# Hybrid DeltaNet, pooling and expert block on one core: input transposed raw as it lands, output products grouped by shape

## The chip, the core and the metric

The kernel runs on one core of a Trainium2 chip. The number that counts is the device time of one execution in microseconds, as the median of several runs. The profile of one execution gives what each engine did: TensorE (PE, with its weight loads as PEld), VectorE (DVE), ScalarE (ACT), GpSimd (POOL), and SyncE (SP), which only issues transfers here.

## What is computed

`x` is 512 tokens by 1024 values, float32. The parts of the reference that the change touches are the first norm and projection, and the output of the scan:

```python
h = _rmsnorm(x, attn_norm_w[l])        # x * rsqrt(mean(x*x) + eps) * w
proj = h @ w_in[l]                     # 1024 -> 2568: q, k, v, z, two gates, pool input
...
def step(state, inp):                  # 8 chunks of 64 tokens, 4 heads of 128
    qd, kd, u_c, w_c, qk_c, gt = inp
    v_new = u_c - jnp.einsum('bhid,bhde->bhie', w_c, state)
    o = jnp.einsum('bhid,bhde->bhie', qd, state) + jnp.einsum('bhij,bhje->bhie', qk_c, v_new)
    state = state * gt[..., None, None] + jnp.einsum('bhid,bhie->bhde', kd, v_new)
    return state, o
```

Before the scan, q, k and v go through a causal convolution of 4 taps, silu and norms, and a unit lower triangular 64x64 matrix per head and chunk is inverted (the "transposed inverse" below is kept as tiles TR and TM and built in 5 levels). Behind the scan come an output norm and gate, the output projection `w_out`, a second norm, a router that picks 4 of 32 experts for each token, the experts (1024 -> 2048 -> 1024 with a clamped SwiGLU), the weighted sum and a last norm.

## The kernel before

Everything is float32 apart from the gather matrices of the experts. Each engine has its own hand-written program; the order of the calls in the code is the order on the engine, and semaphores tie the engines together. SP's queue carries all loads.

**Start.** SP issues the four loads of `x` (128 tokens each, into `xs`), then seven small loads of parameters into the 61 rows of `prow` (norm weight, four rows of convolution taps, two more), and then the weights of the input projection in pieces of 1 MB. ACT sums the squares of each block of tokens (L566) and takes one root for all four (L568). DVE first builds masks for the inverse (L786 to L803: six of them, `lvl`, and `icnt`), copies the transposed parameters out of PSUM (`pcol`, L806), inverts the roots (L808), and scales the four blocks of x into `xn` (L810). PE transposes the parameters (L1235) and then, once all four blocks are scaled, `xn` in 32 tiles of 128x128 (L1240), eight PSUM banks of 512 tokens. ACT (L572) and DVE (L813) share the eight copies out of PSUM and multiply by the norm weight of each row: that is `hT`, the transposed normed input.

**Projections and inverse.** `project(m)` (L1256) multiplies 8 weight tiles of 128x128 with the 8 rows of `hT` into bank 0 or 1, m = 0 to 19. Ahead of `project(0)` stands `four_chunks` (L1285), the two gates of each head, whose sums by chunk follow at L1453. ACT copies a projection out with the first tap (L576, `tap`), DVE adds three taps (L831, `conv`), ACT applies silu (L581). The gates go through a chain of small operations on DVE (L852 to L870) with exponentials and a logarithm on ACT (L645 to L651). The products and the levels of the inverse stand between the projections on PE, written out by hand.

**Scan.** For chunks n = 1 to 7 PE runs `state_values(n)` (L1376), `outputs(n - 1)` and `state_change(n)` (L1390) with quarters of projections between them. DVE subtracts (`values`, L970), updates the state (`state`, L983 and L985) and adds the decayed part to the output (`output`, L996); ACT copies the other part of the output (`keep_intra`, L632). `outputs(n)` makes for each of four heads two products: the queries with the state (L1405: 128 rows of contraction, 64 columns of weights) and the chunk's own scores with the new values (L1406: 64 rows, 64 columns). They alternate head by head. Each float32 product is two instructions in the trace.

**Tail.** Output projection (L1276), second norm, router, then the loop over blocks of 32 tokens of one expert: gather (L1603), gate and up (L1641), down (L1662), with 1 MB units of weights in a ring of 20 slots that SP refills as PE frees them. One unit of the ring is filled early wherever the scan has given its place back.

Of the kernel before, what the change touches and what calls it, by code (L numbers as in the profile page):

```python
# [18 lines left out]
P = 128  # L19
D = 1024  # L20
T = 512
TB = T // P
KD = D // P
H = 4
CONV = 4
# [26 lines left out]
def moe_block(nc, x, attn_norm_w, w_in, conv_w, a_log, dt_bias, dn_norm_w, pool_w, pool_scale, w_out,  # L52
# [3 lines left out]
    with ctx:  # L56
# [66 lines left out]
        catT = cat[:, :].rearrange("p (k t) -> p k t", k=KD)  # L123
        xn = cat[:, :].rearrange("p (b d) -> p b d", b=TB)
        DX = cat[:, 0:1024].rearrange("p (c f) -> p c f", c=NC)
# [92 lines left out]
        def bc(v, n, at):  # L218
# [11 lines left out]
            "iota_ok", "const_ok", "lvl_ok", "pool_step", "pool_mix", "bias_ok")]  # L230
        std_ok, xn_ok, pcol_ps, pcol_ok, xt_ps, ht_even, ht_odd = [sem(n) for n in (
            "std_ok", "xn_ok", "pcol_ps", "pcol_ok", "xt_ps", "ht_even", "ht_odd")]
        proj_ps, tap_ok, conv_ok, silu_ok, ba_ps, dve_step = [sem(n) for n in (
# [83 lines left out]
        def _(sp):  # L317
            def param(row, n, src):
                sp.dma_start(prow[row:row + n, :], src).then_inc(par_in, 16)
# [3 lines left out]
            param(NANW, KD, attn_norm_w.rearrange("l (k p) -> (l k) p", p=P))  # L323
            for j in range(CONV):
                param(NCV + NQKV * j, NQKV, conv_w[0, j:j + 1, :].rearrange("l (k p) -> (l k) p", p=P))
            param(NDN, 1, dn_norm_w)
            param(NPS, 4, pool_scale.rearrange("l (k p) -> (l k) p", p=P))

            w_in_v = w_in[0].rearrange("(k p) c -> p k c", p=P)
# [227 lines left out]
        def _(act):  # L557
# [3 lines left out]
            def row(v):  # L561
                return v.rearrange("p a t -> p (a t)")

            for b in range(TB):
# [209 lines left out]
        def _(dve):  # L774
# [3 lines left out]
            def step(ins, s, count):  # L778
# [17 lines left out]
                                        op0=ALU.mult, op1=ALU.subtract))  # L796
            for s in range(1, LEVELS + 1):
# [4 lines left out]
            link(V.tensor_scalar(icnt[:, :], iotaf[:, 0:PAD], 1.0, None, ALU.add))  # L802
            step(V.reciprocal(icnt[:, :], icnt[:, :]), lvl_ok, 1)  # L803

            dve.wait_ge(pcol_ps, 1)
            step(V.tensor_copy(pcol[:, :], ps[:, 7, 0:61]), pcol_ok, 1)  # L806
            dve.wait_ge(std_ok, 1)
            link(V.reciprocal(sm[:, 8:12], sm[:, 4:8]))  # L808
            for b in range(TB):
                V.tensor_scalar(xn[:, b, :], xs[:, b, :], sm[:, 8 + b:9 + b], None, ALU.mult).then_inc(xn_ok, 1)  # L810
            for k in range(1, KD, 2):
                dve.wait_ge(xt_ps, k + 1)
                V.tensor_scalar(hT[:, k, :], bank(k), pcol[:, NANW + k:NANW + k + 1], None, ALU.mult).then_inc(ht_odd, 1)  # L813

# [24 lines left out]
            for hh in range(2):  # L839
                r = slice(CH * hh, CH * (hh + 1))  # L840
                link(V.tensor_copy(bch[r], bcr[r, 0:2 * H].rearrange("p (k a b) -> p k a b", k=2, a=2)[:, :, :, hh]))
            dve.wait_ge(part_ps, 1)
            V.tensor_copy(ba_part, bank(6)).then_inc(part_ok, 1)
            conv(0)

            dve.wait_ge(ba_ps, 1)
# [384 lines left out]
        def _(pe):  # L1231
            mm, tr = nc.tensor.matmul, nc.tensor.transpose
            pe.wait_ge(const_ok, 6)
            pe.wait_ge(par_in, 16 * (3 + CONV))
            tr(ps[:, 7, 0:61], prow[:, :], ident[0:61, 0:61]).then_inc(pcol_ps, 1)  # L1235
            pe.wait_ge(pcol_ok, 1)
            pe.wait_ge(xn_ok, TB)
            for k in range(KD):
                for b in range(TB):
                    last = tr(bank(k)[:, b * P:(b + 1) * P], xn[:, b, k * P:(k + 1) * P], ident)  # L1240
                last.then_inc(xt_ps, 1)
            pe.wait_ge(ht_even, KD // 2)
            pe.wait_ge(ht_odd, KD // 2)

            def project(m, lo=0, hi=KD):

                piece = m // 2
                if lo == 0:
                    if m % 2 == 0:
                        pe.wait_ge(win_in[piece % 3], (piece // 3 + 1) * 16)  # L1250
                    if 2 <= m < NQKV + 2:
                        pe.wait_ge(conv_ok, m - 1)
                    elif m >= NQKV + 2:
                        pe.wait_ge(silu_ok, m - 1)
                for k in range(lo, hi):
                    last = mm(bank(m % 2), win[:, piece % 3, k, m % 2 * P:(m % 2 + 1) * P], hT[:, k, :], start=k == 0,  # L1256
                              stop=k == KD - 1)
                if hi == KD:
                    last.then_inc(proj_ps, 1)
# [133 lines left out]
            def outputs(n):  # L1393

                if n == 0:
                    pe.wait_ge(u_ok, 4)
                    pe.wait_ge(qkt_ok, 2)
                else:
                    pe.wait_ge(vn_ok, n)
                    pe.wait_ge(o_ok, n)  # L1400
                for hp in range(2):
                    for hh in range(2):
                        c, h = 2 * n + hp, 2 * hp + hh
# [30 lines left out]
            def h2_transposed(b):  # L1434
# [3 lines left out]
                for half in range(2):  # L1438
# [5 lines left out]
                    last.then_inc(h2t_ps, 1)  # L1444

            pe.wait_ge(wba_in, 16)
            four_chunks(bank(6), wba, hT, part_ps)
            project(0)
            pe.wait_ge(const_ok, 7)
# [5 lines left out]
            last.then_inc(ba_ps, 1)  # L1455
            project(1)
            project(2)
# [240 lines left out]
```

## Time and profile before

| | us |
|---|---|
| median of 3 runs | 1402.07 (1401.7 to 1402.2) |
| profiled execution, its own time | 1397.82 |
| its span in the trace | 1396.0 |
| mean granted clock of TensorE | 0.965 of full |
| PE busy | 1272.8 (91%) |
| DVE busy | 504.8 (36%) |
| ACT busy | 289.1 (21%) |
| POOL busy | 159.5 (11%) |

The profiled execution has 1.82 us around its span, and lies 4.25 us under the median of the timed runs. Times in the trace count from the start of the span. The stages: x and norm to 21 us, projections and inverse to 190 us, scan to 254 us, output projection and second norm to 313 us, router to 353 us, experts to about 1350 us, sum and last norm to the end. A busy share says little for such a kernel, since each stage has another limit; what counts is which wait or engine ends last in the stage.

### The profile page before, as it was taken

The numbers are of one execution on the slowest core, as the hardware profiler recorded it, in microseconds if no ns is written. First come the engines' busy times: TensorE is split into PE (matmuls) and PEld (weight loads), VectorE is DVE, ScalarE is ACT, GpSimd is POOL, SyncE is SP. The second block draws the span as 40 slices with busy tenths as digits, with TensorE's granted clock in tenths as the row PEclk, the third lists the DMA queues.
The fourth block names the chain that finished last, engine by engine and source line by source line (L and its number), as shares of the span: only waits on it lengthen the run. The fifth ranks groups of instructions, "written<-read, shape, count | busy, mean of one in ns | idle before, by whom it ended". The sixth has DMA issues, their size and how long they took to land.

```text
span 1396.0 us, 52461 instructions
## 1 busy us (share of the span) xinstructions
PE 1272.8 (91%) x21747; PEld 750.5 (54%) x21747; DVE 504.8 (36%) x1624; ACT 289.1 (21%) x494; POOL 159.5 (11%) x256
## 2 busy tenths in 40 slices
PE   5999999983998999999999999999999999988860
PEld 3446654441555665566565556556566656554440
DVE  5454223226333333333333333333333333332227
ACT  3431123123111111211121112121121112111102
POOL 3100420006000001100010101010010001100000
PEclk9999999995999999999999999999999999999985
DMA  6212140418199999999999999999999999999956
GB/s 209 78 61 62 31 165 32 151 37 352 60 410 416 406 417 407 417 405 418 398 403 417 401 417 407 417 406 417 405 401 417 394 418 404 417 419 417 416 199 293
DMA packets 94579, 447.27 MB, mean 320 GB/s; under 512 B 10973, under 2 KB 22706, under 8 KB 61194
## 3 DMA queue, kind: packets, MB, share of 16 engines
q1 hardware_dynamic: 90778, 437.34, 77.8%
q0 software_dynamic: 3696, 8.40, 1.6%
q8 instruction: 82, 1.34, 0.4%
q14 instruction: 23, 0.19, 0.0%
HBM read 432.52 MB, written 14.88 MB: 320 GB/s over the span
## 4 chain that ended last, share of the span: by engine, by line
PE 69%; DMA 25%; DVE 4%; issue 1%; ACT 0%; SPq 0%; DVEq 0%; POOLq 0%; ACTq 0%
PE ps L1641 27%; DMA ring<-in_w_gate_up_dram 16%; PE ps L1662 13%; PE ps L1256 10%; DMA ring<-in_w_down_dram 8%; PE ps L1603 5%; PE ps L1276 4%; PE ps L1323 1%; DVE ring L1217 1%; PE ps L1634 1%; PE ps L1653 1%; PE ps L1406 1%; PE ps L1612 1%; PE ps L1405 1%; DMA ring<-pair_rows_dram 1%
## 5 line engine op out<-in xcount | busy, mean ns | idle before, releaser
L1641 PE MATMUL ps<-ring,cat 128*32 128x256 f32 x9856 | 555.1, 383 | 15.9 <-DMA ring<-in_w_gate_up_dram 15.9
L1641 PEld LDWEIGHTS ps<-ring,cat 128*32 128x32 f32 x9856 | 311.1, 111 | 231.2 <-DMA ring<-in_w_gate_up_dram 20.7
L1662 PE MATMUL ps<-ring,cat 128*32 128x256 f32 x4928 | 282.4, 379 | 3.6 <-DMA ring<-in_w_down_dram 3.4
L1662 PEld LDWEIGHTS ps<-ring,cat 128*32 128x32 f32 x4928 | 146.0, 110 | 111.1 <-DMA ring<-in_w_down_dram 7.9
L1256 PE MATMUL ps<-hbuf,ring 128*128 128x512 f32 x320 | 145.6, 601 | 0.0
L757 ACT ACTIVATE cat<-cat 128x128 f32<-128x128 f32 x154 | 48.0, 312 | 451.5 <-DVE cat L1198 451.5
L551 POOL DMA_INDIRECT pair_rows_dram<-cat,rowi x77 | 76.9, 999 | 527.6 <-ACT cat L761 527.6
L1182 DVE TENSOR_REDUCE wslot<-ps 128x2 f32<-128x6 f32 x77 | 12.6, 164 | 311.4 <-ACT cat L761 311.0
L761 ACT ACTIVATE cat<-ps,wslot 128x256 f32<-128x256 f32 x77 | 36.7, 477 | 368.2 <-PE ps L1662 368.2
L1603 PE MATMUL ps<-hbuf,cat 128*32 128x256 bf16 x2496 | 108.8, 274 | 3.7 <-DVE cat L1165 3.7
L1198 DVE TENSOR_SCALAR cat<-ps 128x128 f32<-128x128 f32 x154 | 44.9, 291 | 172.7 <-PE ps L1641 171.2
L757 ACT ACT_TABLE_LOAD x77 | 98.8, 1283 | 15.7 <-issue 14.3
L1256 PEld LDWEIGHTS ps<-hbuf,ring 128*128 128x128 f32 x320 | 58.4, 190 | 66.4 <-issue 65.2
L1603 PE MATMUL ps<-aux,cat 128*32 128x256 bf16 x1248 | 90.5, 274 | 0.0
L1603 PEld LDWEIGHTS ps<-hbuf,cat 128*32 128x32 bf16 x2496 | 69.8, 98 | 19.7 <-issue 4.2
L547 POOL TENSOR_TENSOR rowi<-rowj,qcol 128x1 int32<-128x1 int32 x77 | 14.2, 184 | 395.0 <-DMA pair_rows_dram<-cat,rowi 381.6
L1276 PE MATMUL ps<-ring,cat 128*128 128x512 f32 x128 | 56.6, 595 | 2.3 <-DVE ring L1065 1.4
L1165 DVE TENSOR_TENSOR cat<-iotaf,rank 128x512 bf16 x78 | 54.0, 692 | 12.5 <-DVE gie L1161 12.5
L1160 DVE COPY selu<-E 96x32 bf16 x78 | 13.9, 178 | 123.4 <-issue 123.4
L1202 DVE SCALAR_TENSOR_TENSOR cat<-cat 128x128 f32<-128x128 f32 x154 | 45.1, 293 | 19.0
L1206 DVE STREAM_TRANSPOSE cat<-cat 128x128 f32<-128x128 f32 x154 | 48.0, 311 | 5.2
L1205 DVE TENSOR_TENSOR cat<-cat 128x128 f32<-128x128 f32 x154 | 44.9, 292 | 5.2
(300 smaller groups left out, 817.3 us busy)
## 6 DMA issues: line engine op xcount, KB each, us to landing
ring<-in_w_gate_up_dram SPq DMA_DIRECT2D x256, 1024.0 KB, 10.0
ring<-in_w_down_dram SPq DMA_DIRECT2D x128, 1024.0 KB, 10.0
ring<-in_w_in_dram SPq DMA_DIRECT2D x10, 1024.0 KB, 5.8
ring<-pair_rows_dram SPq DMA_DIRECT2D x4, 2048.0 KB, 14.6
ring<-in_w_out_dram SPq DMA_DIRECT2D x1, 4096.0 KB, 12.8
ring<-in_x_dram SPq DMA_DIRECT2D x4, 512.0 KB, 4.9
x_rows_dram<-ring SPq DMA_DIRECT2D x1, 2048.0 KB, 16.3
ring<-x_rows_dram SPq DMA_DIRECT2D x4, 512.0 KB, 6.6
```

What stands on the lines that cost most here:

```text
L551: G.indirect_dma_start(out=pair_rows, out_offset=bass.IndirectOffsetOnAxis(ap=rowi[:, 0:1], axis=0), in_=ys, in_offset=None, bounds_check= ...
L757: A(sg[:, half], gc[:, half], ACT.Sigmoid, scale=ALPHA).then_inc(sg_ok, 1)
L1165: step(V.tensor_tensor(hot[:, :, :, :], slots, mine, ALU.is_equal), hot_ok, count)
L1198: V.tensor_scalar(gc[:, half], ps[:, b, 0:P], LIMIT, None, ALU.min).then_inc(gc_ok, 1)
L1202: step(V.scalar_tensor_tensor(out=uc[:, half], in0=uc[:, half], scalar=1.0, in1=gc[:, half], op0=ALU.add, op1=ALU.mult), uc_step, n * 2 + 2)
L1205: step(V.tensor_tensor(act_[:, half], uc[:, half], sg[:, half], ALU.mult), act_ok, n + 1)
L1206: V.transpose(actT[:, half], act_[:, half]).then_inc(actt_ok, 1)
L1256: last = mm(bank(m % 2), win[:, piece % 3, k, m % 2 * P:(m % 2 + 1) * P], hT[:, k, :], start=k == 0, stop=k == KD - 1)
L1276: last = mm(bank(n % 2), catT[:, k, b * P:(b + 1) * P], wout[:, k, 512 * half:512 * (half + 1)], start=i == 0, stop=i == KD - 1)
L1603: last = mm(ps[SLOTS * q:SLOTS * (q + 1), 2, 0:QD].rearrange("p (j i) -> p j i", i=SLOTS), hot[:, b, 0, :], rows, start=b == 0 and n == 0, ...
L1641: last = mm(ps[SLOTS * q:SLOTS * (q + 1), gu_bank(half), 0:2 * P].rearrange("p (s j i) -> p s j i", s=2, j=4), xgT[:, SLOTS * u:SLOTS * (u ...
L1662: last = mm(ps[SLOTS * q:SLOTS * (q + 1), 1, 0:QD], actT[:, c // 4, SLOTS * (c % 4):SLOTS * (c % 4 + 1)], w[:, i, q * QD:(q + 1) * QD], st ...
```

## The change

Two places of the scan and the start are written anew; the arithmetic is the same up to the order of two multiplications. The norm's scale used to be multiplied into x ahead of the transposes. Now x is transposed as it stands, block by block as the loads land; the norm's weight is multiplied in by the copies out of PSUM (ACT six rows, DVE two), and the norm's scale, which varies along the columns of `hT`, is made a row in PSUM bank 7 by a product of ones with a diagonal matrix (`xdiag`), and multiplied into the eight rows of `hT` by DVE. `project(0)` starts on each row as it is ready, and now stands ahead of `four_chunks`. The small loads go to ACT's queue, as four. Masks of levels 2 to 5 move behind on DVE. In `outputs` the four products with the state come first, and then the four of the chunk.

```diff
         @block.sync
-            param(NANW, KD, ...); four of NCV; param(NDN, ...); param(NPS, ...)
...
         @block.scalar
+            param(NANW, KD, attn_norm_w.rearrange("l (k p) -> (l k) p", p=P))
+            param(NCV, CONV * NQKV, conv_w[0].rearrange("j (k p) -> (j k) p", p=P))
+            param(NDN, 1, dn_norm_w)
+            param(NPS, 4, pool_scale.rearrange("l (k p) -> (l k) p", p=P))
+            act.wait_ge(const_ok, 2)
+            link(A(sm[:, 8:9], epsc[:, 0:1], ACT.Sqrt))
             for b in range(TB):
                 act.wait_ge(x_in[b], 16)
                 link(A(junk, xs[:, b, :], ACT.Square, accum_out=sm[:, b:b + 1]))
-            act.wait_ge(const_ok, 2)
-            A(sm[:, 4:8], sm[:, 0:4], ACT.Sqrt, scale=1.0 / D, bias=epsc[:, 0:1]).then_inc(std_ok, 1)
+                A(sm[:, 4 + b:5 + b], sm[:, b:b + 1], ACT.Sqrt, scale=1.0 / D, bias=epsc[:, 0:1]).then_inc(std_ok, 1)
             act.wait_ge(pcol_ok, 1)
-            for k in range(0, KD, 2):
+            for k in range(2, KD):
                 act.wait_ge(xt_ps, k + 1)
-                A(hT[:, k, :], bank(k), ACT.Copy, scale=pcol[:, NANW + k:NANW + k + 1]).then_inc(ht_even, 1)
+                A(hT[:, k, :], bank(k if k < KD - 1 else 2), ACT.Copy, scale=pcol[:, NANW + k:NANW + k + 1]).then_inc(hraw_ok, 1)
...
         @block.vector
+            def rstd_diagonal(b):
+                dve.wait_ge(const_ok, 3)
+                dve.wait_ge(std_ok, b + 1)
+                link(V.reciprocal(sm[:, 8 + b:9 + b], sm[:, 4 + b:5 + b]))
+                V.tensor_scalar(xdiag[:, b, :], ident, sm[:, 8 + b:9 + b], None, ALU.mult).then_inc(xdiag_ok, 1)
+            rstd_diagonal(0)
+            rstd_diagonal(1)
             dve.wait_ge(pcol_ps, 1)
             step(V.tensor_copy(pcol[:, :], ps[:, 7, 0:61]), pcol_ok, 1)
-            for b in range(TB):
-                V.tensor_scalar(xn[:, b, :], xs[:, b, :], sm[:, 8 + b:9 + b], None, ALU.mult).then_inc(xn_ok, 1)
+            rstd_diagonal(2)
+            for k in range(2):
+                dve.wait_ge(xt_ps, k + 1)
+                step(V.tensor_scalar(hT[:, k, :], bank(k), pcol[:, NANW + k:NANW + k + 1], None, ALU.mult), hraw2_ok, k + 1)
+            rstd_diagonal(3)
+            dve.wait_ge(rrow_ps, 1)
+            for k in range(KD):
+                if k >= 2:
+                    dve.wait_ge(hraw_ok, k - 1)
+                V.tensor_tensor(hT[:, k, :], hT[:, k, :], bank(7), ALU.mult).then_inc(ht_ok, 1)
...
         @block.tensor
+            for b in range(TB):
+                pe.wait_ge(x_in[b], 16)
+                for k in range(KD - 1):
+                    last = x_transposed(b, k, k)
+                    if b == TB - 1:
+                        last.then_inc(xt_ps, 1)
+                if b == 1:
+                    pe.wait_ge(par_in, 16 * 4)
+                    tr(ps[:, 7, 0:61], prow[:, :], ident[0:61, 0:61]).then_inc(pcol_ps, 1)
+            for b in range(TB):
+                pe.wait_ge(xdiag_ok, b + 1)
+                last = mm(bank(7)[:, b * P:(b + 1) * P], ones, xdiag[:, b, :], start=True, stop=True)
+            last.then_inc(rrow_ps, 1)
+            pe.wait_ge(hraw_ok, 1)
+            for b in range(TB):
+                last = x_transposed(b, KD - 1, 2)
+            last.then_inc(xt_ps, 1)
...
+                if n:
+                    for hp in range(2):
+                        for hh in range(2):
+                            mm(bank(7, 4)[rows(hh), hp], chunk_of(qs, n, 2 * hp + hh), state_of(n, hh, hp), start=True, stop=True)
                 for hp in range(2):
                     for hh in range(2):
-                        if n:
-                            mm(bank(7, 4)[rows(hh), hp], chunk_of(qs, n, h), state_of(n, hh, hp), start=True, stop=True)
                         last = mm(bank(7, 4)[rows(hh), 2 + hp], QKT[rows(hh), c, :], UU[rows(hh), c, :], start=True, stop=True)
```

PE at the start of the program, before: one transpose of the parameters, the 32 of the scaled input, the gates' `four_chunks` (L1285), and `project(0)` (the first L1256).

```order
L1235 MATMUL ps<-ring 128x61
L1240 MATMUL ps<-ring,cat 128x128 x32
L1285 MATMUL ps<-hbuf,ring 32x512 x8
L1256 MATMUL ps<-hbuf,ring 128x512 x8
L1453 MATMUL ps<-ring 64x4 x16
L1256 MATMUL ps<-hbuf,ring 128x512 x24
```

PE at the same place now: L1252 are the transposes of the raw input, L1263 that of the parameters, L1268 the row of the norm's scale, L1288 the projections, L1317 the gates.

```order
L1252 MATMUL ps<-ring 128x128 x14
L1263 MATMUL ps<-ring 128x61
L1252 MATMUL ps<-ring 128x128 x14
L1268 MATMUL ps<-cat,ring 128x128 x4
L1252 MATMUL ps<-ring 128x128 x4
L1288 MATMUL ps<-hbuf,ring 128x512 x8
L1317 MATMUL ps<-hbuf,ring 32x512 x8
L1288 MATMUL ps<-hbuf,ring 128x512 x8
L1488 MATMUL ps<-ring 64x4 x16
```

The transposes stand in two runs with the parameters' between them, the last row of `hT` (4 transposes) comes behind the scale's row, and `project(0)` has passed the gates.

DVE at the start now, behind the first level's mask: L808 and L809 are the reciprocal and diagonal of a block, L814 the copy of the parameters, L818 the two rows of `hT` that DVE takes out of PSUM, L824 the eight multiplications by the scale's row.

```order
L809 TENSOR_SCALAR cat<-ring,sm 128x128
L814 COPY pcol<-ps 128x61
L808 RECIPROCAL sm<-sm 128x1
L809 TENSOR_SCALAR cat<-ring,sm 128x128
L818 TENSOR_SCALAR hbuf<-ps,pcol 128x512 x2
L808 RECIPROCAL sm<-sm 128x1
L809 TENSOR_SCALAR cat<-ring,sm 128x128
L824 TENSOR_TENSOR hbuf<-hbuf,ps 128x512 x8
```

The eight scalings of `hT` are new on DVE and stand behind the last block's diagonal; the four wide scalings of x are gone.

PE in the scan, chunk n = 2, before: L1376 is `state_values(2)`, then `outputs(1)` alternates, then a quarter of a projection.

```order
L1376 MATMUL ps<-aux,ring 64x128 x4
L1405 MATMUL ps<-aux,ring 64x128
L1406 MATMUL ps<-ring 64x128
L1405 MATMUL ps<-aux,ring 64x128
L1406 MATMUL ps<-ring 64x128
L1405 MATMUL ps<-aux,ring 64x128
L1406 MATMUL ps<-ring 64x128
L1405 MATMUL ps<-aux,ring 64x128
L1406 MATMUL ps<-ring 64x128
L1256 MATMUL ps<-hbuf,ring 128x512 x2
```

The same place now, where L1408 is `state_values`, L1436 the products with the state and L1440 those of the chunk.

```order
L1408 MATMUL ps<-aux,ring 64x128 x4
L1436 MATMUL ps<-aux,ring 64x128 x4
L1440 MATMUL ps<-ring 64x128 x4
L1288 MATMUL ps<-hbuf,ring 128x512 x2
```

The same eight products stand there, with one change of shape between them in place of seven, and the first four have the shape of `state_values` ahead of them.

## Rows read from the trace of the kernel before

**Rows 1.** Page, part 4: shares of the chain that ended last, by engine

```profile
PE 69%; DMA 25%; DVE 4%; issue 1%; ACT 0%; SPq 0%; DVEq 0%; POOLq 0%; ACTq 0%
```

**Rows 2.** Stages; columns: stretch, length, PE, PEld, DVE, ACT, POOL busy (count), clock, DMA, GB/s

```profile
60.00:100.00 40.00, 40.00 (x208) 20.09 (x207) 24.98 (x36) 16.33 (x24) 1.90 (x1) 1.00 0.17 53
...
400.00:1350.00 950.00, 918.28 (x18720) 556.26 (x18716) 327.31 (x1241) 173.99 (x292) 86.20 (x146) 0.99 0.99 405
```

**Rows 3.** Chain of waits in order of time; columns: start us, us, what

```profile
384.71 11.10 DMA ring<-in_w_down_dram
```

**Rows 4.** Timeline of the start; columns: start us, us, engine, line, operation, [idle before]

```profile
4.50 1.06 ACT L566 ACTIVATE ring<-ring 128x1024 f32<-128x1024 f32 x1 [2.42 <-DMA ring<-in_x_dram]
...
5.34 0.41 SPq L333 DMA_DIRECT2D ring<-in_w_in_dram  x1
...
8.49 1.06 ACT L566 ACTIVATE ring<-ring 128x1024 f32<-128x1024 f32 x1 [0.24 <-DMA ring<-in_x_dram]
...
9.66 1.28 ACT L568 ACT_TABLE_LOAD   x1
...
9.87 0.33 PE L1235 MATMUL ps<-ring 61*128 61x61 f32 x1 [9.87 <-DMA ring<-in_pool_scale_dram]
...
11.57 2.74 DVE L810 TENSOR_SCALAR cat<-ring,sm 128x1024 f32<-128x1024 f32 x4
...
15.64 0.69 ACT L572 ACTIVATE hbuf<-ps,pcol 128x512 f32<-128x512 f32 x1 [4.39 <-PE ps L1240]
```

**Rows 5.** Chain of waits, transposes, gates and first projections; columns as in Rows 3

```profile
14.46 5.36 PE ps L1240 x28
...
21.13 1.92 PE ps L1285 x16
23.05 7.06 PE ps L1256 x16
30.12 1.03 PE ps L1453 x32
```

**Rows 6.** Transposes of L1240 alone; columns: stretch, length, PE busy (count), PEld, clock

```profile
16.40:17.40 1.00, 1.00 (x6) 1.00 (x6) 1.00 1.06 378
18.40:19.40 1.00, 1.00 (x9) 1.00 (x8) 1.00 1.08 364
```

**Rows 7.** Chain of waits, transposes of the second norm's output; columns as in Rows 3

```profile
279.62 0.87 PE ps L1443 x8
...
313.41 3.65 PE ps L1443 x16
```

**Rows 8.** Stages around a pause of PE; columns as in Rows 2

```profile
312.00:313.00 1.00, 0.00 (x0) 0.00 (x0) 1.00 (x2) 1.00 (x3) 0.81 (x1) 0.66 1.03 246
313.00:314.00 1.00, 0.59 (x3) 0.62 (x4) 0.86 (x2) 1.00 (x3) 1.00 (x1) 0.50 1.05 418
```

**Rows 9.** Timeline, DVE and ACT later in the program; columns as in Rows 4

```profile
33.72 0.17 DVE L855 TENSOR_TENSOR ring<-ring 128x16 f32<-128x16 f32 x1
...
39.04 2.32 DVE L831 SCALAR_TENSOR_TENSOR ring<-ps,pcol,ring 128x511 f32<-128x511 f32 x3 [5.14 <-ACT ring L576]
...
264.89 1.27 DVE L1065 TENSOR_TENSOR ring<-ring,ps 128x512 f32<-128x512 f32 x2
```

**Rows 10.** Timeline of the scan, chunks 1 and 2; columns as in Rows 4

```profile
192.74 0.66 PE L1376 MATMUL ps<-aux,ring 128*64 128x128 f32 x8
193.32 0.65 PE L1406 MATMUL ps<-ring 64*64 64x128 f32 x8
193.91 1.99 PE L1256 MATMUL ps<-hbuf,ring 128*128 128x512 f32 x4
...
198.38 0.66 PE L1376 MATMUL ps<-aux,ring 128*64 128x128 f32 x8
198.87 0.38 PE L1405 MATMUL ps<-aux,ring 128*64 128x128 f32 x2
...
201.71 1.98 PE L1256 MATMUL ps<-hbuf,ring 128*128 128x512 f32 x4
```

More of the change, by code:

```diff
@@ L230, in moe_block @@
             "iota_ok", "const_ok", "lvl_ok", "pool_step", "pool_mix", "bias_ok")]
[L231 to L232 removed]
+        std_ok, xdiag_ok, pcol_ps, pcol_ok, xt_ps, ht_ok, hraw_ok, hraw2_ok, rrow_ps = [sem(n) for n in (
+            "std_ok", "xdiag_ok", "pcol_ps", "pcol_ok", "xt_ps", "ht_ok", "hraw_ok", "hraw2_ok", "rrow_ps")]
         proj_ps, tap_ok, conv_ok, silu_ok, ba_ps, dve_step = [sem(n) for n in (
@@ L562, in row, with param @@
                 return v.rearrange("p a t -> p (a t)")
+            def param(row, n, src):
+                act.dma_start(prow[row:row + n, :], src).then_inc(par_in, 16)
+            param(NANW, KD, attn_norm_w.rearrange("l (k p) -> (l k) p", p=P))
[4 more added lines that the diff above has]
+            link(A(sm[:, 8:9], epsc[:, 0:1], ACT.Sqrt))
             for b in range(TB):
@@ L796, in _, with level_mask @@
                                         op0=ALU.mult, op1=ALU.subtract))
-            for s in range(1, LEVELS + 1):
+            def level_mask(s):
                 link(V.tensor_scalar(row_i, spare_i, s, None, ALU.logical_shift_right))
@@ L801, in _ @@
                 link(V.tensor_tensor(lvl[:, s, :], lvl[:, s, :], identC, ALU.add))
-            link(V.tensor_scalar(icnt[:, :], iotaf[:, 0:PAD], 1.0, None, ALU.add))
-            step(V.reciprocal(icnt[:, :], icnt[:, :]), lvl_ok, 1)
+            level_mask(1)
+            def rstd_diagonal(b):
[5 more added lines that the diff above has]
+            rstd_diagonal(1)
             dve.wait_ge(pcol_ps, 1)
             step(V.tensor_copy(pcol[:, :], ps[:, 7, 0:61]), pcol_ok, 1)
-            dve.wait_ge(std_ok, 1)
-            link(V.reciprocal(sm[:, 8:12], sm[:, 4:8]))
-            for b in range(TB):
-                V.tensor_scalar(xn[:, b, :], xs[:, b, :], sm[:, 8 + b:9 + b], None, ALU.mult).then_inc(xn_ok, 1)
-            for k in range(1, KD, 2):
-                dve.wait_ge(xt_ps, k + 1)
-                V.tensor_scalar(hT[:, k, :], bank(k), pcol[:, NANW + k:NANW + k + 1], None, ALU.mult).then_inc(ht_odd, 1)
+            rstd_diagonal(2)
+            for k in range(2):
+                dve.wait_ge(xt_ps, k + 1)
+                step(V.tensor_scalar(hT[:, k, :], bank(k), pcol[:, NANW + k:NANW + k + 1], None, ALU.mult), hraw2_ok, k + 1)
[5 more added lines that the diff above has]
+                V.tensor_tensor(hT[:, k, :], hT[:, k, :], bank(7), ALU.mult).then_inc(ht_ok, 1)
             def turned(a):
@@ L844, in _ @@
             conv(0)
+            level_mask(4)
+            level_mask(5)
+            link(V.tensor_scalar(icnt[:, :], iotaf[:, 0:PAD], 1.0, None, ALU.add))
+            step(V.reciprocal(icnt[:, :], icnt[:, :]), lvl_ok, 1)
             dve.wait_ge(ba_ps, 1)
@@ L1232, in _, with x_transposed @@
             mm, tr = nc.tensor.matmul, nc.tensor.transpose
+            def x_transposed(b, k, to):
+                return tr(bank(to)[:, b * P:(b + 1) * P], xs[:, b, k * P:(k + 1) * P], ident)
+            pe.wait_ge(const_ok, 3)
+            for b in range(TB):
[7 more added lines that the diff above has]
+                    tr(ps[:, 7, 0:61], prow[:, :], ident[0:61, 0:61]).then_inc(pcol_ps, 1)
             pe.wait_ge(const_ok, 6)
-            pe.wait_ge(par_in, 16 * (3 + CONV))
-            tr(ps[:, 7, 0:61], prow[:, :], ident[0:61, 0:61]).then_inc(pcol_ps, 1)
             pe.wait_ge(pcol_ok, 1)
[L1237 to L1243, printed above, removed]
+            for b in range(TB):
[6 more added lines that the diff above has]
+            last.then_inc(xt_ps, 1)
             def project(m, lo=0, hi=KD):
@@ L1444, in h2_transposed @@
                     last.then_inc(h2t_ps, 1)
+            project(0)
             pe.wait_ge(wba_in, 16)
             four_chunks(bank(6), wba, hT, part_ps)
-            project(0)
+            project(1)
             pe.wait_ge(const_ok, 7)
```

16 lines of the change are left out of this document (6 added, 10 removed).

## The prediction

> **What bounds the kernel now.** I read the shares of the chain of waits first, then the stages, then the timelines of the two places that the change touches. The chain is PE 69%, DMA 25%, DVE 4% [rows 1], so a microsecond taken from PE counts where PE is never idle. From 60 to 100 us it is busy 40.00 of 40.00 us with DMA at 0.17 [rows 2], and the stages between 60 and 230 us look the same. The experts are set by the weights: from 400 to 1350 us DMA is 0.99 busy at 405 GB/s [rows 2], and PE first waits for them at 384.71 [rows 3]. Nothing anchors that stream to the clock on the wall. The loads ahead of it are released by PE's progress, and the refills by slots that PE has used, so what PE wins before 384 us moves the whole stream forward. I pass gains on in full.
>
> The start is another chain: ACT squares the last block at 8.49, needs a table load of 1.28 at 9.66, DVE scales four blocks from 11.57 for 2.74 [rows 4], PE transposes from 14.46, and its first projection work is the gates at 21.13 [rows 5]. PE does nothing but the parameters' transpose for the first 14.4 us.
>
> **The start, step by step.** The first block is there at 4.50, the others about 1.33 apart ((8.49 - 4.50) / 3) [rows 4]. Seven transposes for each block: what does one cost? The same form costs 0.87 / 8 = 0.11 us late in the program and 3.65 / 16 = 0.23 after a pause [rows 7], where the granted clock has fallen to 0.50 [rows 8]. In the first stage the clock column reads 1.00, but the starts tell otherwise: 6 in a microsecond at 16.4, 9 at 18.4 [rows 6]. So PE began at its lower level (1.2 GHz) and rose to 2.4 GHz while it transposed, some four us after 14.46. With 0.23 each: block 0 from 4.6 to 6.2, block 1 to 7.8, parameters 0.33 [rows 4] to 8.1, then the rise about 8.6 (four us of transposes again), block 2 to 9.2, and block 3 from 9.2 to 10.0. Its first row is out at about 9.5.
>
> ACT has squares and a root for each block now. From the last square to the table load before was 9.66 - 8.49 = 1.17, and from the end of that load to DVE's scaling, less a reciprocal of 0.2, 0.4 [rows 4]. A cycle of square and root is thus 1.4, the last block's square starts at 4.50 + 3 x 1.4 = 8.7, and its root is done at 10.2. The table load is gone from the path, since one set serves both. ACT then copies six rows at 0.69 [rows 4], from 10.2 to 15, always ahead of DVE.
>
> DVE is what ends last. It takes rows 0 and 1 out of PSUM (0.75 each with the wait between: 9.6 to 11.2) and then makes the last diagonal. That operation is not in the trace: it lies between a small one of 0.17 [rows 9] and one of 1024 columns at 2.74 / 4 = 0.69 [rows 4]; 128 columns are nearer to the small one, 0.25. With the reciprocal it is 11.7. The product of ones and diagonal is 0.4 with its latency (0.33 for the parameters' transpose): 12.15. The first multiplication of `hT`, 0.64 by L1065 (1.27 for two, same shape) [rows 9], ends at 12.9, and `project(0)` starts at 12.95. Eight take 5.1 us, and PE needs 7.06 for `project(0)` [rows 5], so PE sets the pace from there: 20.0, gates 1.92 [rows 5] to 21.9. Before, the same two ended at 30.12. **Term 1: 8.2 us.**
>
> Its bounds: were DVE free at 10.2, the chain root, diagonal, product, first row would give 11.8, so 9.3. At the other end, the parameters might land where they did before, at 9.87 [rows 4]. They are issued far earlier, by ACT ahead of its work (four issues of some 0.4 before 4.50, which cost nothing unless they outlast the load), but beside x and not behind it. PE would stand 2.1 us ahead of block 2 and `project(0)` would start some 2.7 later: 5.5.
>
> Covers. The first weights were issued at 5.34 [rows 4] and now about 2.7, behind x on the same queue; 1 MB at 400 GB/s behind 8.4 is 11.0, needed at 12.95. The masks of levels 2 and 3 (8 operations of about 0.25) lie between DVE's last row, 17.3, and the gates at 21.9; those of 4 and 5 behind conv(0), until 27.7, while the gate sums come at 30.0. All have about 2 us of cover.
>
> **A wait that tightens.** The gates' sums used to stand ahead of `project(1)` (30.12, 1.03) [rows 5], and stand behind it now: 28.9 to 30.0. ACT waits in its order for the small gate operations before it copies `project(1)` out. Four operations at 0.2 [rows 9] and three short exponentials: 31.5; copy 0.69: 32.2; three taps 2.32 [rows 9]: 34.6. `project(3)`, which needs that bank, is due at 37.0. So 2.4 us are left, and nothing is lost. If they are not enough, every further microsecond counts in full.
>
> **The scan, step by step.** Eight instructions of one shape behind another shape: L1406 from 193.32 to 193.91, 0.59. L1376 from 192.74 to 193.32, 0.58; followed by its own shape it takes 198.38 to 198.87, 0.49. The alternating block takes 198.87 to 201.71, 2.84 [rows 10], for 16 instructions of the same two kinds. Grouped: L1376 and the state's products 0.49 + 0.58, chunk products 0.59, together 1.66 in place of 3.33. That is 1.67 for each of six, and for `outputs(7)`, which follows a wide product, 0.58 + 0.59 in place of 2.84, 1.67 again. **Term 2: 7 x 1.67 = 11.7 us.** Does the recurrence allow it? A round is now 1.66, a quarter projection 1.98 [rows 10], state change 0.7, a quarter 1.98: about 6.1. The state change ends at 4.3, DVE's update of 128x512 takes 0.64 to 0.69, so the state is there near 5.1, a microsecond ahead. Bounds of the term: 7.0, if that microsecond is short by 0.7 a round, to 12.5.
>
> **Sum.** 8.2 + 11.7 = 19.9. The profiled execution took 1397.82 (span 1396.0 and 1.82 around it), so the changed kernel would show a span of 1376.1 and 1377.9 for itself. The median lies 4.25 above the profiled one, so 1402.07 - 19.9 = 1382.2.
>
> **Rivals.**
> A, a poorer start: PE falls back to its lower level before `project(0)`, or the parameters come late. After 10.0 it has a pause of a microsecond, small products, and another pause. It fell at 312 to 313 us after a stage with no matmul at all [rows 8], and the gap before 21.13, of about one microsecond, did not slow L1256 (7.06 for 16) [rows 5], which speaks against. If it falls, or has not risen, four us at half speed cost 2; late parameters 2.7. Time 1384.2 to 1384.9.
> The Trainium skill, "TensorE: Matmul & The Clock Gate", part 4 (PE-mode transpose), says that transposes do not raise the clock as other products do; by it `project(0)` would begin at the lower level, which is this rival at about 1384.2. The trace disagrees, since the rate rose within a run of nothing but transposes.
> B, the alternation is not what costs: the products with the state wait for something that the order does not change. Against it stand the two grouped rows of the same shapes at 0.58 and 0.59 [rows 10]. Time 1402.07 - 8.2 = 1393.9, half of it 1388.
> C, the tightened gate chain or the recurrence ends last, by 2 to 5 us: 1384 to 1387.
> D, the gain is hidden: the expert stream starts when it did, for a load that nothing moved. Against it, DMA is 0.17 busy at 60 to 100 us [rows 2], so it has room to keep up. Time near 1402.
> E, slower: PE begins with transposes in small groups as blocks land and stays at 1.2 GHz into the projections, where the whole path is PE. Half speed costs one microsecond for each two in which it holds; with 19.9 to lose, it decides after 40 us (12.95 to 53), and if it held to 77 us the time would be 1414. Against it: an uninterrupted `project(0)` of 7 us.
>
> **How the numbers follow.** Forecast 0.62, A 0.18, B 0.07, C 0.07, D 0.03, E 0.03. The forecast's own case reaches from 1380.3 (9.3 + 12.5) to 1384; with A and C the range is 1380.3 to 1387.5. B in full, D and E are left out. A measurement of this kernel tells about 0.2%, 2.8 us, from no change. Faster holds the forecast, A, B and C, 0.94; same D, 0.03; slower E, 0.03.
>
> **What would show it.** In the changed profile: first transpose at about 4.6, seven a block at 0.23 and later 0.11; the first multiplication by the scale's row at 12.2; `project(0)` at 12.95 and 7.1 long; gates' end at 21.9; `project(3)` without a gap. In the scan the products L1436 and L1440 in 0.58 and 0.59, no wait of PE for the state, and a distance of 1.66 from `state_values` to the next projection. The first wait for weights at 384.7 - 19.9 = 364.8. Wrong would be: a first projection after 15, an L1288 of twice the length, a gap ahead of L1408, or a stream that starts later than 365.

## The result and the profile after

| | before | after |
|---|---|---|
| median of the timed runs, us | 1401.88 (1400.74 to 1402.2, 4 runs) | 1377.76 (1375.22 to 1381.79, 4 runs) |
| ratio, 95% interval | | 0.9832 (0.9805 to 0.9859) |
| profiled execution, us | 1397.82 | 1376.16 |
| span, us | 1396.0 | 1374.4 |
| PE busy, us | 1272.8 | 1258.6 |

The change makes the kernel faster by 1.7%: 24.1 us by these medians, 21.7 by the two profiled executions. Forecast were 19.9 us and 1382.2, with a range from 1380.3, so the time came out 2.5 us below the range. The mechanism and both terms of the sum hold to 0.4 us; what was wrong is how a median was made from them, and how narrow the range was.

The start of the changed kernel in the chain of waits (start us, us, what), beside [rows 5]: L1252 are transposes of raw x, L1263 of the parameters, L818 the two rows that DVE takes out of PSUM, L809 the last diagonal, L1268 the scale's row, L824 the first multiplication with it, L1288 the projections, L1317 the gates.

```profile
4.62 3.44 PE ps L1252 x14
8.06 0.29 PE ps L1263
8.36 1.45 PE ps L1252 x8
9.83 0.76 DVE hbuf L818
10.62 0.76 DVE hbuf L818
11.40 0.17 DVE sm L808
11.60 0.30 DVE cat L809
11.94 0.50 PE ps L1268 x2
12.46 0.70 DVE hbuf L824
13.30 7.10 PE ps L1288 x16
20.41 1.85 PE ps L1317 x16
22.26 7.07 PE ps L1288 x16
29.32 1.03 PE ps L1488 x32
```

The chain is the one that was forecast, link by link: DVE's own queue ends last (9.83 to 12.46), and `project(0)` starts at 13.30 (forecast 12.95). The second projection starts at 22.26; before, projection work stood at the same point at 30.12 [rows 5]. Term 1 is 30.12 - 22.26 = 7.9 us (forecast 8.2).

The scan, timeline, chunks 1 and 2 (start us, us, engine, line, operation), beside [rows 10]; L1408 is `state_values`, L1436 the products with the state, L1440 those of the chunk:

```profile
190.72 0.66 PE L1408 MATMUL ps<-aux,ring 128*64 128x128 f32 x8
191.21 0.61 PE L1436 MATMUL ps<-aux,ring 128*64 128x128 f32 x8
191.75 0.65 PE L1440 MATMUL ps<-ring 64*64 64x128 f32 x8
192.33 1.98 PE L1288 MATMUL ps<-hbuf,ring 128*128 128x512 f32 x4
194.25 0.71 PE L1422 MATMUL ps<-ring 64*128 64x128 f32 x8
```

From `state_values` to the next projection it is 192.33 - 190.72 = 1.61 us (forecast 1.66, before 3.33). No wait of PE for the state appears: the only two from 20 to 290 us, 0.9 and 1.4 us, are ahead of products of the output projection and stood there before with the same lengths (then L1276).

```profile
PE ps L1308 <- DVE ring L1082: 1.4, 1, 1.4
PE ps L1308 <- issue: 0.9, 1, 0.9
```

Chain of waits at the end of the output projection (DVE's last addition), before:

```profile
308.88 0.70 DVE ring L1065
```

and after, with the first wait for weights, which stood at 384.71 before [rows 3]:

```profile
289.21 0.70 DVE ring L1082
...
365.10 10.53 DMA ring<-in_w_down_dram
```

The last addition came at 308.88 in the trace before and comes at 289.21: 19.7 us, 7.9 from the start and 11.8 from the scan (forecast 11.7). The first wait for weights moved by 384.71 - 365.10 = 19.6; 364.8 had been written. So in this pair of traces the gain passes through the second norm, the router and the first experts in full. The place of that first wait is partly luck: the chain of another execution of the changed kernel first waits at 375.53, for a later unit of weights. The other 2.0 us between the two profiled executions (21.7 in the time) arise behind 365 us, where the change touches nothing, and 2.4 more between the medians. That remainder is what the experiments had to explain.

### The profile page after: what moved, and what is told of

Its sections match the earlier page's. It is cut to its first block, busy times and chain, and to the rows that moved or that the text cites. A ratio compares the mean times of both kernels' runs of the same rounds, so it can differ in the third digit from the quotient of the medians.

```text
span 1374.4 us, 52489 instructions
## 1 busy us (share of the span) xinstructions
PE 1258.6 (92%) x21755; PEld 740.7 (54%) x21755; DVE 507.1 (37%) x1633; ACT 288.6 (21%) x499; POOL 159.7 (12%) x256
## 4 chain that ended last, share of the span: by engine, by line
PE 60%; DMA 34%; DVE 4%; issue 2%; SPq 0%; POOL 0%; ACT 0%; DVEq 0%; POOLq 0%; ACTq 0%
PE ps L1675 22%; DMA ring<-in_w_gate_up_dram 21%; DMA ring<-in_w_down_dram 12%; PE ps L1696 11%; PE ps L1288 10%; PE ps L1637 4%; PE ps L1308 4%; PE ps L1355 1%; DVE ring L1234 1%; PE ps L1668 1%; PE ps L1687 1%; DMA ring<-pair_rows_dram 1%; PE ps L1646 1%; PE ps L1348 1%; DMA pair_rows_dram<-cat,rowi 0%
## 5 line engine op out<-in xcount | busy, mean ns | idle before, releaser
L1675 PEld LDWEIGHTS ps<-ring,cat 128*32 128x32 f32 x9856 | 306.1, 110 | 233.2 <-DMA ring<-in_w_gate_up_dram 20.7
L1696 PEld LDWEIGHTS ps<-ring,cat 128*32 128x32 f32 x4928 | 145.9, 110 | 112.7 <-DMA ring<-in_w_down_dram 9.0
L1288 PE MATMUL ps<-hbuf,ring 128*128 128x512 f32 x320 | 145.8, 601 | 0.4 <-DVE hbuf L824 0.4
L1288 PEld LDWEIGHTS ps<-hbuf,ring 128*128 128x128 f32 x320 | 58.3, 190 | 66.5 <-issue 64.9
L1637 PEld LDWEIGHTS ps<-hbuf,cat 128*32 128x32 bf16 x2496 | 69.2, 98 | 19.9 <-issue 4.2
```

Source lines behind the costliest of these rows:

```text
L1637: last = mm(ps[SLOTS * q:SLOTS * (q + 1), 2, 0:QD].rearrange("p (j i) -> p j i", i=SLOTS), hot[:, b, 0, :], rows, start=b == 0 and n == 0, ...
L1675: last = mm(ps[SLOTS * q:SLOTS * (q + 1), gu_bank(half), 0:2 * P].rearrange("p (s j i) -> p s j i", s=2, j=4), xgT[:, SLOTS * u:SLOTS * (u ...
L1696: last = mm(ps[SLOTS * q:SLOTS * (q + 1), 1, 0:QD], actT[:, c // 4, SLOTS * (c % 4):SLOTS * (c % 4 + 1)], w[:, i, q * QD:(q + 1) * QD], st ...
```

## The experiments

**Theory S**: the change is worth its front, 19.6 us, and the rest is the spread of executions. **Theory R**: the weight stream is really shorter in the changed kernel, for a cause in its code or in the phase at which the experts start. Each run is compared with the kernel before on the same chip.

**The kernel before, against itself.** No edit.

> The kernel before, against itself. Theory S (the front of the program gained 19.6 us, as its trace shows, and the other 2 to 4 us of the measured gain come from how long the weight stream of the experts happens to take in each execution): the difference to the reference runs is 0 with single executions spread by 2 to 7 us, and in the trace the wait for the first missing weights at 384.7 is reached within 0.2 us while the stretch from there to the last expert's scaled output (967.0 us in the first profile) differs by microseconds. Theory R (the stream is really shorter in the changed kernel): this one is steady within 1 us, at 1401 to 1402, and its stream takes 967 to 971.

Measured: 1398.09 us (1396.96 to 1401.48, 12 runs) against 1398.28 (1396.33 to 1403.1, 23 runs), ratio 0.9995 (0.9983 to 1.0007). The same program is spread over 7 us. The 1402 of the first session lies near the upper end, and the profiled 1397.82 in the middle. R's condition, steady at 1401 to 1402, is not met. The first expert also took longer in this trace. Its chain, after the kernel before's own:

```profile
353.44 6.91 PE ps L1641 x124
```

```profile
353.60 8.87 PE ps L1641 x103
```

Its first wait for weights comes at 386.84 and not at 384.7. So S's own expectation, that everything up to that wait repeats within 0.2 us, is wrong as well: part of the spread lies ahead of it.

**The changed kernel again.** No edit.

> The changed kernel once more. Theory S: its first wait for weights is again at 365.1 within 0.2 us, the stream from there varies between about 964 and 971 us, and over five rounds the gain settles at 19.6 plus or minus 2: ratio 0.984 to 0.9875. Theory R: the gain stays at 24, ratio 0.983 or lower.

Measured: 1377.52 us (1375.72 to 1381.12, 5 runs), ratio 0.9848 (0.9829 to 0.9867), a gain of 20.8 us. That is within what S expected (0.984 to 0.9875); R's 0.983 is at the very edge of the interval. In the trace S missed: the first wait for weights in the chain stands at 375.53 and not at 365.1, although the last addition (288.95) and the first expert (333.50) come 0.3 us earlier than in the first trace. Another unit of the stream is the first to be waited for; from the last addition to the last expert's scaled output the two traces have 1041.1 and 1042.8 us. Of the 12 traces of this study six first wait for the unit of [rows 3], and six for a later one.

**The changed kernel, held back.** 184 idle transposes ahead of the first projection:

```diff
-            pe.wait_ge(hraw_ok, 1)
+            pe.wait_ge(hraw_ok, 2)
             for b in range(TB):
                 last = x_transposed(b, KD - 1, 2)
             last.then_inc(xt_ps, 1)
+            for i in range(184):
+                tr(bank(3)[:, 0:P], xs[:, 0, 3 * P:4 * P], ident)
```

> The changed kernel with 184 more transposes of x (results unused) on TensorE ahead of the first projection, 184 x 0.109 = 20.1 us, so that its front is as long as before. Theory S: 0.5 us slower than the kernel before, within the spread of executions, 1400 to 1404. Theory R, with a cause in the changed code (another queue for the small loads, another order in the scan): it stays 2 to 4 us under the kernel before. R with a cause in the phase in which the experts start: equal to the kernel before.

Measured: 1399.14 us (1397.89 to 1400.53, 12 runs) against 1398.28, ratio 1.0001 (0.9992 to 1.001). (S's window, 1400 to 1404, was written against a reference of 1402.) The last addition of this trace comes at 310.18, against 308.88 before. With the front made long again the new code has no advantage left. A faster stream from the new code (the small loads on another queue, the order of the scan) is excluded down to 1 or 2 us: the interval reaches to 1.1 us under the kernel before, and S expected 0.5 us above it. An effect of the phase is not excluded by this run; the repetition leaves little for it to explain, since its gain of 20.8 us (18.6 to 23.9 by the interval) holds the 19.6 of the front.

**The start alone.** The changed kernel with the old loop in `outputs`:

```diff
-                if n:
-                    for hp in range(2):
-                        for hh in range(2):
-                            mm(bank(7, 4)[rows(hh), hp], chunk_of(qs, n, 2 * hp + hh), state_of(n, hh, hp), start=True, stop=True)
                 for hp in range(2):
                     for hh in range(2):
+                        if n:
+                            mm(bank(7, 4)[rows(hh), hp], chunk_of(qs, n, h), state_of(n, hh, hp), start=True, stop=True)
                         last = mm(bank(7, 4)[rows(hh), 2 + hp], QKT[rows(hh), c, :], UU[rows(hh), c, :], start=True, stop=True)
```

> The new start with the old alternating order in outputs. By the trace of the changed kernel the first term is 30.12 - 22.26 = 7.9 us: the second projection starts at 22.3, the scan is as long as before, the first wait for weights comes at 384.7 - 7.9 = 376.8. Theory S: 1394 plus or minus 2. Theory R: 1390 to 1392.

Measured: 1390.99 us (1390.47 to 1391.82, 6 runs), ratio 0.9939 (0.9925 to 0.9953), a gain of 7.3 where 7.9 was the trace's. The absolute time falls into R's window and not S's, but only because the expectation was written against a reference of 1402 again, and on this chip it is 1398.3; the difference is S's. The second projection starts at 22.22, as expected; the first wait for weights in the chain is that for a later unit, at 391.20 and not 376.8. The trace held something new. The last addition came at 302.88 and not at 308.88 - 7.9 = 301.0. Stages of this trace (stretch, length, PE, PEld, DVE, ACT, POOL busy, granted clock, DMA, GB/s), behind the sums of squares, a block of 64 one-column products:

```profile
118.00:120.00 2.00, 2.00 (x72) 1.93 (x69) 0.69 (x1) 0.67 (x2) 0.00 (x0) 1.00 0.41 91
120.00:122.00 2.00, 2.00 (x63) 1.99 (x62) 1.46 (x3) 0.47 (x1) 0.00 (x0) 0.99 1.06 375
122.00:124.00 2.00, 2.00 (x3) 0.72 (x3) 1.38 (x2) 0.55 (x1) 0.00 (x0) 0.50 0.21 66
124.00:126.00 2.00, 2.00 (x4) 0.84 (x3) 0.00 (x0) 0.08 (x1) 0.00 (x0) 0.66 0.00 0
```

PE is busy 2.00 of 2.00 throughout, and yet its granted clock falls from 2.4 to 1.2 GHz for some three microseconds, from small products on, and half a projection takes 5.33 in place of 3.63 us in the chain. In the changed kernel's first trace the same place stays at 1.00:

```profile
122.00:124.00 2.00, 2.00 (x5) 0.81 (x5) 1.42 (x2) 0.51 (x1) 0.00 (x0) 1.00 0.20 66
```

The dip stands in 4 of the 12 traces of this study, in four different kernels, always at this place of the program, and costs 1.7 us each time.

**The scan alone.** The kernel before with the new `outputs` (the edit above, reversed):

> The old start with the grouped outputs. If the changes of shape are what the alternation costs, each of outputs(1) to (7) goes from 2.84 to 1.1 or 1.2 us and the last addition of the output projection, at 308.9 before, ends its chain at 297.1: 11.7 us earlier, time 11 to 13 us under the kernel before. If the products with the state wait for something else, 0 to 6 us. The two halves of the change should add up: 7.3 measured for the start alone, 20.8 for both, so 13.5 left, of which the trace explains 11.8 and the spread of executions the rest.

Measured: 1386.77 us (1385.87 to 1388.91, 5 runs), ratio 0.9922 (0.9908 to 0.9935), a gain of 11.2. Timeline, last addition of this kernel:

```profile
297.19 0.69 DVE L1065 TENSOR_TENSOR ring<-ring,ps 128x512 f32<-128x512 f32 x1 [6.18 <-PE ps L1276]
```

That is 308.88 - 297.19 = 11.7 us earlier, as the sum had it. The two halves give 7.3 + 11.2 = 18.5 of measured time beside 20.8 for both (the scan alone was measured on another chip than the other two, each against the kernel before there); the traces give 7.9 + 11.7 = 19.6. They add up within the spread; the 13.5 that I had expected here by difference was not met.

**What the alternation costs: groups of two.**

```diff
-                if n:
-                    for hp in range(2):
-                        for hh in range(2):
-                            mm(bank(7, 4)[rows(hh), hp], ...)
                 for hp in range(2):
+                    if n:
+                        for hh in range(2):
+                            mm(bank(7, 4)[rows(hh), hp], ...)
                     for hh in range(2):
...
```

> The changed kernel with outputs in four groups of two products (state, chunk, state, chunk): three changes of shape inside in place of one (grouped) or seven (alternating). If a change of shape costs a fixed (2.84 - 1.17) / 6 = 0.28 us, outputs takes 1.73 and the whole is 7 x 0.56 = 3.9 us slower than the changed kernel. If the cost is that of two neighbouring products of the same kind being kept apart in some other way (loading of weights, for one), it would be nearer to the middle, 2.0, and 5.8 slower.

Measured: 1378.5 us (1378.04 to 1379.69, 4 runs), ratio 0.9857 (0.9842 to 0.9872). Timeline of `outputs(1)`; L1436 are the products with the state, L1439 those of the chunk, and L1288 is the projection behind them:

```profile
190.71 0.39 PE L1436 MATMUL ps<-aux,ring 128*64 128x128 f32 x4
191.03 0.44 PE L1439 MATMUL ps<-ring 64*64 64x128 f32 x4
191.40 0.44 PE L1436 MATMUL ps<-aux,ring 128*64 128x128 f32 x4
191.76 0.44 PE L1439 MATMUL ps<-ring 64*64 64x128 f32 x4
192.13 1.98 PE L1288 MATMUL ps<-hbuf,ring 128*128 128x512 f32 x4
```

Both expectations miss. The block takes 192.13 - 190.71 = 1.42, against 1.12 grouped and 2.84 alternating, so by the trace it is 2.1 us slower over seven chunks and not 3.9 or 5.8. The cost is not a fixed sum for each change of shape: two products between changes take 0.36 to 0.37, about what one takes between changes (2.84 / 8 = 0.355). A run of one shape costs at least 0.36 us here, whether one product or two are in it, and four take 0.58; only the first run of the block, which continues the shape of `state_values`, is shorter (191.03 - 190.71 = 0.32). There one operand and the PSUM bank change and the shape does not, and the price is missing, which speaks for the shape as what counts.

**Do the halves of the array overlap?** Neighbours in that run lie on different halves. Here they are kept apart:

```diff
-                    for hp in range(2):
-                        for hh in range(2):
+                    for hh in range(2):
+                        for hp in range(2):
```

(in both groups)

> The changed kernel with the two halves of the array kept apart in outputs: both products of the upper half, then both of the lower, in each group of four. In the run with four groups of two, a group of two products took 0.36 us, as long as a single product did when they alternated, so either neighbours on different halves overlap, or each run of one shape has a floor of 0.36. If the overlap of halves is what helps, the two groups of four now take longer than 1.12, towards 4 x 0.18 for each group. If only the floor for each run counts, they stay at 1.1.

```profile
193.20 0.66 PE L1436 MATMUL ps<-aux,ring 128*64 128x128 f32 x8
193.78 0.66 PE L1440 MATMUL ps<-ring 64*64 64x128 f32 x8
194.38 1.98 PE L1288 MATMUL ps<-hbuf,ring 128*128 128x512 f32 x4
```

1.18 us in place of 1.12. In runs of four the halves matter by 0.06, and not by the 0.3 that an overlap of halves would have asked for, so what the numbers show is a floor for each run. A run of two products on one half was not made, and what the engine does during the floor stays open. (One execution, 1382.41 us, with the dip of the clock in it.)

**Parameters behind x again.** The changed kernel with the four small loads issued by SP after x:

```diff
+                sp.dma_start(prow[row:row + n, :], src).then_inc(par_in, 16)
...
-                act.dma_start(prow[row:row + n, :], src).then_inc(par_in, 16)
```

> The changed kernel with its four small parameter loads issued by SyncE behind x again and not by ScalarE. Bound of the prediction: they land near 9.9, TensorE stands about 2 us ahead of block 2, project(0) starts at 15 to 16 in place of 13.3. If the loads are quick wherever they are issued, project(0) starts at 13.3 as before.

```profile
4.63 3.25 PE L1253 MATMUL ps<-ring 128*128 128x128 f32 x14 [4.63 <-POOL ring L452]
9.06 0.27 PE L1264 MATMUL ps<-ring 61*128 61x61 f32 x1 [1.19 <-DMA ring<-in_pool_scale_dram]
9.27 1.75 PE L1253 MATMUL ps<-ring 128*128 128x128 f32 x14
...
13.87 4.53 PE L1289 MATMUL ps<-hbuf,ring 128*128 128x512 f32 x10 [0.43 <-DVE hbuf L825]
```

PE waits 1.19 us for the parameters, and `project(0)` starts at 13.87 and not at 15 to 16. The lower bound of term 1 in the prediction (5.5) was too low: the loads, four in place of seven, land at 9.06 even from this queue. 13.87 is only 0.57 us behind the 13.30 of the first trace, but there block 1 of x landed late and the transposes of blocks 2 and 3 took 2.16 us and not 1.75. Counted from the end of ACT's last root, 10.00 here, `project(0)` starts after 3.87 us, against 2.63 to 2.81 in the three traces of the changed kernel: 1.1 to 1.2 us are lost, and not 2.7. One execution: 1380.48 us.

**One row less for DVE.** Row 1 of `hT` is copied by ACT:

```diff
-            for k in range(2, KD):
+            for k in range(1, KD):
                 act.wait_ge(xt_ps, k + 1)
...
-            for k in range(2):
+            for k in range(1):
                 dve.wait_ge(xt_ps, k + 1)
```

(with the waits on `hraw_ok` one higher)

> The changed kernel with one of VectorE's two copies out of PSUM (row 1) given to ScalarE, which has time from 10.5. If VectorE's queue is what ends last at the start, its last reciprocal starts at 10.65 and not at 11.40, and project(0) at 12.5 and not at 13.3: 0.7 us. If the root on ScalarE ends last, no change (its root ends at 10.5, so the two are close). In the time 0.7 us is below what rounds can tell.

Timeline of this kernel:

```profile
10.35 0.29 ACT L567 ACTIVATE sm<-sm,epsc 128x1 f32<-128x1 f32 x1
...
10.77 0.16 DVE L808 RECIPROCAL sm<-sm 128x1 f32<-128x1 f32 x1
10.97 0.28 DVE L809 TENSOR_SCALAR cat<-ring,sm 128x128 f32<-128x128 f32 x1
...
12.67 1.52 PE L1288 MATMUL ps<-hbuf,ring 128*128 128x512 f32 x3 [0.17 <-DVE hbuf L824]
```

`project(0)` starts at 12.67. That start differs between executions of one program: 13.30, 13.04 and 12.80 in the three traces of the changed kernel, with ACT's last root ending at 10.49 in the first. Counted from that root (10.64 here) the first projection comes after 2.03 us, and in the three traces of the changed kernel after 2.81, 2.66 and 2.63: DVE's queue was what ended last, by 0.6 to 0.8 (one trace of this kernel). The time, 1376.35 us (1376.06 to 1377.05, 4 runs), ratio 0.9842 (0.9827 to 0.9857), is the lowest median of the study, but its interval overlaps that of the changed kernel, so that it beats it is not shown by time.

**The changed kernel a third time.** No edit.

> The changed kernel a third time, for its trace: TensorE's granted clock fell to its lower level for some 3 us in a busy stretch behind the sums of squares (one-column products) in 2 of the first 4 experiments' traces and not in the others. If that is chance in each execution, it may or may not show here; the stretch from the last addition of the output projection to the last expert's output is expected between 1041 and 1045 us.

One execution, 1381.07 us, 4.9 us above the first profiled one. Its last addition is earlier than there, at 288.71, and no dip stands at 120 us; its first wait for weights is 2.4 us later. Chain and granted clock of the first expert, in the changed kernel's first trace (chain: start us, us, what; stages of PE alone: stretch, length, PE busy, clock, DMA, GB/s):

```profile
333.77 6.91 PE ps L1675 x96
...
365.10 10.53 DMA ring<-in_w_down_dram
```

```profile
334.00:338.00 4.00, 4.00 (x80) 1.00 0.01 4
```

and in this one:

```profile
333.52 9.59 PE ps L1675 x128
...
367.52 10.37 DMA ring<-in_w_down_dram
```

```profile
334.00:338.00 4.00, 4.00 (x42) 0.50 0.02 4
338.00:342.00 4.00, 4.00 (x72) 0.90 0.00 0
```

The router leaves the clock at 1.2 GHz in both. In the first trace it is back at 2.4 GHz when the first expert starts, here some five microseconds later, and the expert takes 2.7 us more. From the last addition to the last expert's scaled output this trace has 1046.5 us, above the 1045 expected; the others have 1041.1 (changed kernel, first), 1042.8 (second), 1042.9 (before), 1044.8 (before, again), 1041.9 (held back) and 1042.9 (start alone), and the traces of the five other runs 1039.8 to 1045.0. Neither program is at one end of them. Nor is the late return rare: in 6 of the 12 traces the first expert has its 6.91 us, and in the other six, of both programs, 8.44 to 9.59. These six have 1042.3 to 1046.5 us behind the last addition, and the first six 1039.8 to 1042.9.

## Why the prediction was right and wrong

**Right: what bounds the kernel.** PE sets the front and the weights set the experts; a gain ahead of the stream moves the whole of it. The last addition moved by 19.7 and the last expert's scaled output by 21.4 us (1351.73 to 1330.33). That the first wait for weights moved by 19.6, to 365.10 where 364.8 was written, is in part luck: in the other two traces of the changed kernel it stands at 375.53 and 367.52. By the prediction's own words, "a stream that starts later than 365", these would have told against it, and they do not: the sign was badly chosen, since executions differ in which unit is waited for first and in how late the first expert's clock returns.

**Right: the start.** The reading that the clock stood at 1.2 GHz during the first transposes, against the column that says 1.00, gave 8.1 for the end of the parameters' transpose (8.35 measured). ([rows 6] counts the products busy in a stretch and not their starts; the step that it shows is real, since the first 14 transposes now take 3.44 us.) The 0.35 us that `project(0)` came late are 0.23 for DVE's first copy (9.83 and not 9.6) and the rest for the links behind the two copies: reciprocal and diagonal 0.54 and not 0.5, the product 0.52 and not 0.45, the first multiplication and the step to PE 0.84 and not 0.8. The last root ended at 10.49 and not at 10.2, but it is not on the path. DVE's queue as the last link is shown by the run with one row less. Six traces have this start: `project(0)` comes at 12.80 to 13.59 in them, so term 1 is known to about 0.5 us.

**Right: the scan.** 1.61 for 1.66, and the recurrence had room (the terms of the round add up to 6.3 us and not to the 6.1 written, which leaves more of it). The forecast came from rows of the same shapes in a group, so it did not need the mechanism, which I had as a price for each change of shape. The runs with two in a group showed a floor for each run instead.

**Right: the tightened gate chain, and no rival in force.** Between 20 and 250 us PE waits only the 0.9 and 1.4 us that it waited before. The clock did not fall ahead of `project(0)`: 7.10 or 7.11 us in the three traces of the changed kernel, 7.06 before. The rule of the Trainium skill, "TensorE: Matmul & The Clock Gate", part 4 (PE-mode transpose), that transposes do not raise the clock as other products do, would have made it longer; the trace does not bear it out.

**Wrong: the step from the profiled execution to the median.** "The median lies 4.25 above the profiled one, so 1402.07 - 19.9 = 1382.2" took an offset from three runs as a property of the kernel. It is none: in 23 runs of the kernel before in the next session the median is 1398.28, 0.5 from the profiled 1397.82, and the changed kernel's median in the first session lies 1.6 above its profiled execution. With that, 1398.28 - 19.9 = 1378.4, and the changed kernel has 1377.76 and 1377.52. The sum was good to a microsecond, and the reference was four off.

**Wrong: the range.** Its lower end, 1380.3, held the bounds of the two terms and no term for the spread of executions, which reaches 7 us for one and the same program. Three runs within 0.5 us of each other had looked like a steady kernel. The traces name three parts of the spread: the clock's dip at 120 us (0 or 1.7, in 4 of 12 traces), its return at the first expert (0, or 1.5 to 2.7, in 6 of 12), and the start (0.8: blocks of x land at different times, and the 14 transposes of blocks 2 and 3 take from 1.75 to 2.67 us). The first two are PE's granted clock in stretches that the change does not touch.

What stays open: why the three timed runs of the first session agreed at 1402, when other sessions give 1396 to 1403 with about half of the runs under 1398.3, so that chance, the chip and the session are not told apart; and the microseconds by which the stream itself differs from one execution to the next behind the first wait for weights (965.2 to 967.7 us to the last output in the six traces that first wait for the same unit).

## What to carry to other kernels

When small products of two tile shapes alternate on TensorE, group them: here a run of one shape cost some 0.36 us whether one or two products were in it, and seven blocks of eight products gave back 11.7 us by order alone. A scale that a transpose must wait for can often be multiplied in behind it as a row, so that the transposes use the time in which the loads land; then look for the engine whose own queue now ends last. And make a forecast in differences, from trace to trace; before adding it to a median, ask how far single executions of the same program lie apart, since three runs that agree do not show it; and take as a sign a point that every execution passes, such as the last addition here, and not the first of many waits.

## What the hardware did that was not expected

- TensorE's granted clock fell to 1.2 GHz in a stretch in which the engine was busy without a gap, behind 64x64 tiles and one-column products, in 4 of 12 traces, for 1.7 us of time.
- After the router the clock had come back when the first expert started in 6 of 12 traces, and came back three to five microseconds into it in the other six: 6.91 against 8.44 to 9.59 us for the same products.
- A run of one shape on TensorE had a floor of 0.36 us, so that two small float32 products cost no more than one.
